# Dummy products on TensorE during the routing of a mixture-of-experts layer

## Chip, cores and metric

The kernel runs on one core of a Trainium2 chip. The metric is the device time of one execution in microseconds (us), median of several runs. All tensors are f32.

## What is computed

One decoder layer for 512 tokens of width 1024: a mixing stage (block-sparse attention and an RWKV-7 recurrence), a cross-attention into 256 memory tokens, and a mixture of 32 experts, each followed by a residual and a layer norm. The change lies at the passage from the second norm to the experts:

```python
x = layer_norm(DEEPNORM_ALPHA * x + memory_cross_attention(x, mem, w_mem_q[l], w_mem_kv[l], w_mem_o[l]),
               ln_g[l, 1], ln_b[l, 1])
xf = x.reshape(B * S, D)
e_idx, gate = route(xf, w_router, b_router)     # sigmoid scores; best group of 4; top 2 in it
y = moe_ffn(xf, e_idx, gate.astype(x.dtype), w_exp_gate[l], w_exp_up[l], w_exp_down[l])
x = layer_norm(DEEPNORM_ALPHA * x + y.reshape(B, S, D), ln_g[l, 2], ln_b[l, 2])

def expert_block(args):
    xb, e = args
    h = jax.nn.silu(xb @ w_gate[e]) * (xb @ w_up[e])
    return h @ w_down[e]
```

Each expert's three matrices are 2 MB each, 6 MB in all, so 192 MB of weights pass through the core.

## The kernel before

**The routing block** (L1638 to L1843). TensorE multiplies the output projection of the cross-attention (L1709, 64 products of 128x128 weights with 512 columns), turns the normed tokens (L1692, `tokens`), multiplies them with the router (L1699, `logits`) and turns the 32 x 512 logits (L1726). VectorE then picks the group and the two experts of each token (L1780 to L1811; its result is `oh`, signalled by `oh_done`). TensorE counts with two products how many tokens stand before each one in its expert's list (L1731, L1732, `rk_full`). VectorE makes the weights of the two experts (L1814 to L1821), the place of each token in its expert's list (L1828 to L1834) and the 0/1 matrix `hit` (L1384, `hits_done`). TensorE multiplies that in eight products of 96 columns, the table product (L1390), and VectorE copies the result to `tabs` (L1397 to L1399): for each expert, up to 64 token numbers, row numbers and weights. This ends the block for TensorE and VectorE. SyncE has issued expert loads meanwhile: experts 0, 1 and 2 have a buffer each, filled by then.

**The expert block** (L1920 on). SyncE loads the norm's parameters (L175, two loads), then the weights from expert 3 on, in halves of 1 MB (`load_half`, L1419). A load may be issued when TensorE has read the same part of the expert three before (`w_read`, L1931) and when the fourth load before it has landed (L1933). The first half of expert 3's gate and up weights thus waits for the first half of expert 0's gate and up products. GpSimd clears a buffer (L1983), gathers the 64 rows of an expert (L1969) and later scatters its results (L1974). TensorE, for each expert e: 32 instructions of gate and up products (L2042, in two halves of 16), transposes of the next expert's tokens (L2026, L2027), transposes of the hidden values (the same lines), and 16 instructions of the down projection (L2051). The last expert's result is not scattered but added by products (L2125).

The names used below: `bank[7]` is an accumulation bank that is free between the copy of L1772 and the transposes of L2086; `x1` holds the normed tokens, `ident` a unit matrix.

Of the kernel before, what the change touches and what calls it, by code (L numbers as in the profile page):

```python
# [54 lines left out]
def hybrid_decoder_trunk(nc, x, x_t, mem_t, params, w_in, w_decay_up, w_iclr_up, w_gate_up, w_out, w_mem_q, w_mem_kv, w_mem_o, w_router,  # L55
                         b_router, w_exp_gate, w_exp_up, w_exp_down, ln_g, ln_b, out):
    ctx = ExitStack()
    with ctx:
        def sb(name, shape, dt=F32):
            return ctx.enter_context(nc.sbuf_tensor(name, shape, dt))  # L60
# [14 lines left out]
        def link(eng, ins):  # L75
# [9 lines left out]
        bank = ([tpair[:, i, :] for i in range(2)] + [cpair[:, i, :] for i in range(2)]  # L85
                + [ctx.enter_context(nc.psum_tensor(f"bank{i}", [P, 512], F32)) for i in range(4, 8)])

        ident = sb("ident", [P, P])
# [31 lines left out]
        x1 = keys[:, :, :, :].rearrange("p a j s -> p (a j s)").rearrange("p (t d) -> p t d", t=NT)  # L121
# [7 lines left out]
        def slot(g, width):  # L129
            s = slot_of(g)  # L130
            buf = avq[:, :] if s == 2 else ring[:, s * SLOT:(s + 1) * SLOT]
            return buf[:, 0:KT * width].rearrange("p (k n) -> p k n", k=KT)
# [26 lines left out]
        def group_here(eng, g):  # L159
            eng.wait_ge(w_here[slot_of(g)], 16 * uses_of_slot(g))  # L160
# [48 lines left out]
        with A:  # L209
# [15 lines left out]
            with A1:  # L225
# [55 lines left out]
                with nc.Block() as block:  # L281
                    @block.sync
                    def _(sp):
                        gl = slot(GL, 2 * P)
                        for h, (here, done) in enumerate(((x_here[0], gl_half), (x_here[1], w_here[slot_of(GL)]))):
                            ks = slice(4 * h, 4 * h + 4)
                            sp.dma_start(gl[:, ks, :], groups[GL][:, ks, :]).then_inc(done, 16)
                            sp.dma_start(xT[:, ks, :], x_t[:, ks, :]).then_inc(here, 16)
                        load_group(sp, GK)
                        sp.dma_start(wup[0:64, :], w_decay_up[0]).then_inc(up_here, 16)  # L290
                        sp.dma_start(wup[64:128, :], w_iclr_up[0]).then_inc(up_here, 16)
                        sp.dma_start(wg[:, :], w_gate_up[0]).then_inc(up_here, 16)
                        for g, last in ((GR, ("L", 1)), (GV, ("K", 3)), (GAV, ("R", 3)), (GAQ, ("V", 3))):
                            load_group(sp, g, (job_full, jobs.index(last) + 1))
# [194 lines left out]
            with A2:  # L489
                def s2(name, shape, dt=F32):  # L490
# [52 lines left out]
                         + [("K", i) for i in range(KT // 2)]  # L543
                         + [("V", i) for i in range(2 * MT)])
                fill_units = [(f, part) for f, (kind, _) in enumerate(fills)
                              for part in range(1 if kind in ("bon", "gate") else 8)]
                early_units = sum(fills[f][0] not in ("K", "V") for f, _ in fill_units)
# [43 lines left out]
                for r in range(ROUNDS):  # L591
                    n, k = divmod(r, RPI)
# [795 lines left out]
        def table_product(pe):  # L1388
            for kt in range(TOP_K * NT):
                last = nc.tensor.matmul(bank[6][:, 0:3 * NE], hit[:, kt, :],  # L1390
                                        sel_rows[:, kt // NT, kt % NT, :, :].rearrange("p f e -> p (f e)"),
                                        start=(kt == 0), stop=(kt == TOP_K * NT - 1))
            last.then_inc(tab_full, 1)
# [35 lines left out]
        with B:  # L1429
# [208 lines left out]
            with nc.Block() as block:  # L1638
# [45 lines left out]
                @block.tensor  # L1684
                def _(pe):
                    def tokens(t):

                        pe.wait_ge(n2.shifted, t + 1)
                        for hf in range(2):
                            for k in range(4):  # L1690
                                c = 4 * hf + k
                                last = nc.tensor.transpose(bank[2 * t + hf][:, k * P:(k + 1) * P],  # L1692
                                                           x1[:, t, c:D:KT], ident[:, :])
                            last.then_inc(t2_full, 1)

                    def logits(t):

                        for k in range(KT):
                            last = nc.tensor.matmul(bank[0][0:NE, t * P:(t + 1) * P], wr[:, k, :],  # L1699
                                                    x2T[:, k, t * P:(t + 1) * P], start=(k == 0), stop=(k == KT - 1))  # L1700
                        return last

                    group_here(pe, GMO)
                    group_here(pe, GMO + 1)
                    for t in range(NT):
                        for hf in range(2):
                            w = slot(GMO + hf, 512)
                            for k in range(KT):
                                last = nc.tensor.matmul(bank[2 * t + hf][:, :], omT[:, k, t * P:(t + 1) * P],  # L1709
                                                        w[:, k, :], start=(k == 0), stop=(k == KT - 1))  # L1710
                            last.then_inc(mo2_full, 1)
                        if t >= 2:
                            tokens(t - 2)
                    tokens(NT - 2)
                    pe.wait_ge(router_here, 32)
                    for t in range(NT - 1):
                        pe.wait_ge(t2_act, 2 * t + 2)
                        logits(t)
                    tokens(NT - 1)
                    pe.wait_ge(t2_act, 2 * NT - 1)  # L1720
                    pe.wait_ge(t2_dve, 1)
                    last = logits(NT - 1)
                    last.then_inc(lg_full, 1)
                    pe.wait_ge(lg_read, 1)
                    for t in range(NT):
                        last = nc.tensor.transpose(bank[1][:, t * NE:(t + 1) * NE], lg[:, t * P:(t + 1) * P],  # L1726
                                                   ident[0:NE, 0:NE])
                    last.then_inc(lt_full, 1)

                    pe.wait_ge(oh_done, 1)  # L1730
                    nc.tensor.matmul(bank[2][:, 0:P], before[:, :], oh[:, 2, :, :], start=True, stop=True)  # L1731
                    nc.tensor.matmul(bank[2][:, P:2 * P], ones[:, :], oh[:, 2, :, :], start=True, stop=True)\  # L1732
                        .then_inc(rk_full, 1)
                    pe.wait_ge(hits_done, 1)
                    pe.wait_ge(ids_done, 2)
                    table_product(pe)

                @block.scalar
                def _(act):
# [572 lines left out]
```

## Time and profile before

| what | value |
|---|---|
| median of 3 runs | 1179.37 us (1179.17 to 1180.02) |
| profiled execution | 1179.95 us, its span 1178.1 us |
| TensorE busy (matmul) | 1049.1 us, 89% |
| VectorE, ScalarE, GpSimd busy | 329.5, 244.7, 85.1 us |
| mean granted clock of TensorE | 0.97 |
| DMA moved | 262.83 MB, mean 223 GB/s |
| the chain that ended last | DMA 28%, PE 14%, DVE 2% of the span |

Times in the trace count from the span's start. The routing lies between 629 and 650 us, the expert block behind it.
### The profile page before, as it was taken

What the parts mean: (1) busy time and instruction counts of PE and PEld (TensorE: products, weight loads), DVE (VectorE), ACT (ScalarE), POOL (GpSimd) and SP (SyncE); (2) the same over time, 40 slices, a digit from 0 to 9 for tenths busy, and PEclk for the clock granted to TensorE, in tenths of its full rate; (3) what the DMA queues carried; (4) which work ended last, traced back from release to release, by engine and by line L of the source; (5) the groups of instructions that cost most, each with busy time, mean ns of one, the idle gap of its engine ahead of it and who ended that gap; (6) DMA issues with size and microseconds to landing.
All of it is one profiled execution on the core that took longest, in us unless ns stands there. A gap on an engine that the chain in (4) does not pass through costs nothing. (4 is left out here: it accounts for less than half of the span.)

```text
span 1178.1 us, 15678 instructions
## 1 busy us (share of the span) xinstructions
PE 1049.1 (89%) x6604; PEld 525.7 (45%) x6604; DVE 329.5 (28%) x705; ACT 244.7 (21%) x494; POOL 85.1 (7%) x130
## 2 busy tenths in 40 slices
PE   7999899999899999998995799999987778898876
PEld 3444445567655544565444344434333333333332
DVE  0179522234665453004236100100000000000007
ACT  2431122234445401024001111111110111011112
POOL 2000100000000000000000311111111101111000
PEclk9999899999999999999997799999999999989997
DMA  7112120222104402720309599999999999999994
GB/s 252 47 51 100 70 73 2 73 73 74 42 33 144 179 1 70 286 105 40 112 1 352 221 406 408 401 406 398 400 393 390 397 384 395 389 405 401 400 371 179
DMA packets 55382, 262.83 MB, mean 223 GB/s; under 512 B 7170, under 2 KB 8322, under 8 KB 30352
## 3 DMA queue, kind: packets, MB, share of 16 engines
q1 hardware_dynamic: 50048, 253.39, 55.6%
q0 software_dynamic: 5120, 8.40, 2.2%
q8 instruction: 53, 0.87, 0.3%
q14 instruction: 17, 0.14, 0.0%
q10 hardware_dynamic: 144, 0.02, 0.0%
HBM read 257.60 MB, written 12.58 MB: 229 GB/s over the span
## 5 line engine op out<-in xcount | busy, mean ns | idle before, releaser
L2042 PE MATMUL tpair<-ring,xgT 128*64 128x512 f32 x352 | 82.9, 619 | 13.1 <-DMA ring<-in_w_exp_up 12.4
L2206 DVE TENSOR_TENSOR hb<-cpair,sil 64x512 f32<-64x512 f32 x21 | 14.6, 693 | 276.6 <-ACT sil L2146 276.6
L2042 PE MATMUL cpair<-ring,xgT 128*64 128x512 f32 x352 | 78.9, 595 | 13.7 <-DMA ring<-in_w_exp_up 13.1
L2042 PE MATMUL cpair<-xT,xgT 128*64 128x512 f32 x160 | 71.5, 594 | 15.1 <-DMA ar<-in_w_exp_up 15.1
L2042 PE MATMUL cpair<-ar,xgT 128*64 128x512 f32 x160 | 71.8, 596 | 0.0
L1974 POOL DMA_INDIRECT y_rows<-ye,tabs x32 | 32.5, 1015 | 410.8 <-ACT ye L2154 410.0
L900 PE MATMUL bank<-xT,ring 128*128 128x512 f32 x128 | 60.3, 605 | 0.0
L2042 PEld LDWEIGHTS tpair<-ring,xgT 128*64 128x64 f32 x352 | 27.5, 142 | 67.0 <-issue 66.1
L2042 PEld LDWEIGHTS cpair<-ring,xgT 128*64 128x64 f32 x352 | 26.4, 137 | 64.1 <-issue 63.3
L2154 ACT ACTIVATE ye<-bank,tabs 128x512 f32<-128x512 f32 x31 | 21.3, 687 | 155.2 <-PE bank L2051 155.2
L2051 PE MATMUL bank<-avq,hT 128*64 128x512 f32 x176 | 46.3, 674 | 5.7 <-DVE hT L2210 5.7
L2206 DVE TENSOR_TENSOR hb<-tpair,sil 64x512 f32<-64x512 f32 x11 | 7.6, 693 | 147.1 <-ACT sil L2146 147.1
L2042 PEld LDWEIGHTS cpair<-xT,xgT 128*64 128x64 f32 x160 | 21.0, 137 | 62.0 <-issue 62.0
L345 PE MATMUL bank<-xT,ring 128*128 128x512 f32 x112 | 48.5, 593 | 0.0
L2051 PE MATMUL bank<-ring,hT 128*64 128x512 f32 x176 | 41.8, 618 | 5.7 <-DVE hT L2210 5.7
L2146 ACT ACTIVATE sil<-cpair 64x512 f32<-64x512 f32 x21 | 12.4, 591 | 162.6 <-PE cpair L2042 162.6
L2051 PE MATMUL bank<-mixT,hT 128*64 128x512 f32 x160 | 39.7, 643 | 5.2 <-DVE hT L2210 5.2
L919 PE MATMUL tpair<-ring,mixT 128*128 128x512 f32 x96 | 42.0, 593 | 0.0
L345 PE MATMUL tpair<-xT,ring 128*128 128x512 f32 x64 | 29.5, 621 | 7.8 <-DMA xT<-in_x_t 7.8
L991 ACT ACTIVATE pcb<-tpair 128x512 f32<-128x512 f32 (+1 forms) x32 | 17.4, 544 | 90.0 <-DVE pcb L1159 89.9
L345 PEld LDWEIGHTS bank<-xT,ring 128*128 128x128 f32 x112 | 21.2, 190 | 27.1 <-issue 26.3
L2027 PEld LDWEIGHTS tpair<-ident,xg 64*128 64x128 f32 x224 | 32.5, 225 | 0.0
(389 smaller groups left out, 1619.9 us busy)
## 6 DMA issues: line engine op xcount, KB each, us to landing
ring<-in_w_exp_gate SPq DMA_DIRECT2D x44, 1024.0 KB, 10.1
ring<-in_w_exp_up SPq DMA_DIRECT2D x44, 1024.0 KB, 10.3
ring<-in_w_exp_down SPq DMA_DIRECT2D x22, 1024.0 KB, 11.1
avq<-in_w_exp_down SPq DMA_DIRECT2D x22, 1024.0 KB, 11.2
xT<-in_w_exp_gate SPq DMA_DIRECT2D x20, 1024.0 KB, 11.6
ar<-in_w_exp_up SPq DMA_DIRECT2D x20, 1024.0 KB, 11.2
mixT<-in_w_exp_down SPq DMA_DIRECT2D x20, 1024.0 KB, 11.6
ring<-in_w_in SPq DMA_DIRECT2D x6, 2048.0 KB, 8.2
```

Source lines behind the costliest of these rows:

```text
L345: last = nc.tensor.matmul(dst[:, :], w[:, k, j * P:(j + 1) * P], xT[:, k, :], start=(k == 0), stop=(k == KT - 1))
L900: last = nc.tensor.matmul(dst[:, :], lhs, rhs, start=(k == 0), stop=(k == KT - 1))
L919: last = nc.tensor.matmul(wo_bank[i % 3][:, :], mixT[:, k, t * P:(t + 1) * P], slot(GO + hf, 512)[:, k, :], start=(k == 0), stop=(k == 2 * ...
L991: return nc.scalar.activation(dst, src, ACT.Copy, **kw)
L1974: return pool.indirect_dma_start(y_rows[:, :], bass.IndirectOffsetOnAxis(idx.bitcast(U32), 0), src, None, bounds_check=below(TOP_K * S * 2 ...
L2027: return nc.tensor.transpose(dst, src, ident[0:CAP, 0:CAP])
L2042: last = nc.tensor.matmul(bank[1 + s][m * CAP:(m + 1) * CAP, :], xgT[:, k, :], expert_slot(s, m)[:, k * DE:(k + 1) * DE], start=(k == 0), ...
L2051: last = nc.tensor.matmul(bank[5][m * CAP:(m + 1) * CAP, :], hT[:, k, :], expert_slot(s, 2)[:, o:o + 512], start=(k == 0), stop=(k == FT - 1))
L2146: nc.scalar.activation(sil[:, :], bank[1 + e % 3][0:CAP, :], ACT.Silu).then_inc(sil_done, 1)
L2154: nc.scalar.activation(ye[:, e % 3, :], bank[5][:, :], ACT.Copy, scale=tabs[:, e, 2:3].bitcast(F32)).then_inc(y_scaled, 1)
L2206: V.tensor_tensor(hb[:, :], bank[1 + e % 3][CAP:P, :], sil[:, :], ALU.mult).then_inc(h_done, 1)
```

## The change

TensorE gets three groups of products in the routing block: eight after the transposes of the logits, ahead of its wait for `oh_done`; four after the two counting products, ahead of its waits for `hit` and `sel_rows`; six after the table product, as its last instructions of the block. They multiply `ident` with 512 columns of `x1` into bank 7; nothing reads the result, and the bank is overwritten in the next block.

```diff
                     last.then_inc(lt_full, 1)
 
+                    def kept_busy(n):
+
+                        for _ in range(n):
+                            nc.tensor.matmul(bank[7][:, :], ident[:, :], x1[:, 0, 0:512], start=True, stop=True)
+
+                    kept_busy(8)
                     pe.wait_ge(oh_done, 1)
                     nc.tensor.matmul(bank[2][:, 0:P], before[:, :], oh[:, 2, :, :], start=True, stop=True)
                     nc.tensor.matmul(bank[2][:, P:2 * P], ones[:, :], oh[:, 2, :, :], start=True, stop=True)\
                         .then_inc(rk_full, 1)
+                    kept_busy(4)
                     pe.wait_ge(hits_done, 1)
                     pe.wait_ge(ids_done, 2)
                     table_product(pe)
+                    kept_busy(6)
```

## Rows read from the trace of the kernel before

**Rows 1.** The page, the span in 40 slices: granted clock and DMA share, in tenths.

```profile
PEclk9999899999999999999997799999999999989997
DMA  7112120222104402720309599999999999999994
```

**Rows 2.** Busy time by stretch: length, PE, PEld, DVE, ACT, POOL, clock, DMA share, GB/s.

```profile
633.00:635.00 2.00, 0.00 (x0) 0.00 (x0) 1.79 (x9) 0.00 (x0) 0.00 (x0) 1.00 1.01 414
635.00:636.00 1.00, 0.00 (x0) 0.00 (x0) 0.87 (x4) 0.00 (x0) 0.00 (x0) 0.84 1.04 426
...
645.00:650.00 5.00, 3.73 (x16) 3.49 (x16) 1.62 (x10) 0.00 (x0) 0.00 (x0) 0.50 0.62 259
...
663.00:665.00 2.00, 2.00 (x12) 0.67 (x10) 0.00 (x0) 0.00 (x0) 0.00 (x0) 1.00 0.14 45
```

**Rows 3.** Timeline, routing and expert 0: start, length, engine, line, tiles, idle before.

```profile
631.86 0.43 PE L1726 MATMUL tpair<-ident,lg 32*128 32x32 f32 x4 [0.77 <-DVE lg L1776]
639.85 0.79 PE L1731 MATMUL cpair<-oh,before 128*128 128x128 f32 x2 [7.56 <-DVE oh L1811]
...
645.37 3.73 PE L1390 MATMUL bank<-sel_rows,hit 128*128 128x96 f32 x16 [4.30 <-DVE hit L1384]
...
656.41 0.74 PE L2026 MATMUL tpair<-ident,xg 64*128 64x64 f32 x2 [7.32 <-DMA xg<-xs_rows,tabs]
...
658.59 5.82 PE L2042 MATMUL tpair<-ring,xgT 128*64 128x512 f32 x16 [0.69 <-ACT xgT L2141]
```

**Rows 4.** The SP queue's waits (total us, times, longest), and its timeline.

```profile
SPq L1419 <- PE tpair L2042: 15.8, 2, 13.6
...
664.46 0.33 SPq L1419 DMA_DIRECT2D ring<-in_w_exp_gate  x1
```

**Rows 5.** The chain that ended last, in order of time: start, length, what.

```profile
784.42 6.76 PE tpair L2042 x31
791.18 11.17 DMA ar<-in_w_exp_up
...
1126.17 3.67 PE tpair L2042 x16
```

**Rows 6.** TensorE's timeline: rows at full clock in the shapes of the new products.

```profile
513.56 3.73 PE L1466 MATMUL tpair<-ar,avq 128*128 128x128 f32 x32
...
570.96 7.03 PE L1709 MATMUL tpair<-avq,ar 128*128 128x512 f32 x16
577.83 7.03 PE L1709 MATMUL cpair<-ring,ar 128*128 128x512 f32 x16
```

**Rows 7.** VectorE's timeline in the routing.

```profile
639.50 0.29 DVE L1811 TENSOR_TENSOR oh<-oh 128x128 f32<-128x128 f32 x1
...
642.05 0.09 DVE L1828 MEMSET sc<- 128x32 f32 x1
...
644.09 1.23 DVE L1384 TENSOR_TENSOR hit<-caps,place 128x1024 f32<-128x1024 f32 x1
```

**Rows 8.** The end of the routing block: timeline, and the SP queue's wait.

```profile
649.47 0.20 DVE L1399 COPY tabs<-bank 128x32 f32<-128x32 f32 x1
649.94 0.33 SPq L175 DMA_DIRECT2D kT<-in_ln_g  x1
...
SPq L1638 <- PEq L1638: 10.6, 1, 10.6
```

**Rows 9.** Down projections of experts 26, 30 and 31 (timeline), and the clock there.

```profile
1068.17 5.35 PE L2051 MATMUL bank<-mixT,hT 128*64 128x512 f32 x16 [0.52 <-DVE hT L2210]
...
1132.76 3.65 PE L2051 MATMUL bank<-ring,hT 128*64 128x512 f32 x16 [0.52 <-DVE hT L2210]
...
1146.98 0.68 PE L2026 MATMUL bank<-ident,hb 64*128 64x64 f32 x2 [1.42 <-DVE hb L2206]
...
1148.56 6.59 PE L2051 MATMUL bank<-avq,hT 128*64 128x512 f32 x16 [0.52 <-DVE hT L2210]
...
1148.00:1154.00 6.00, 5.48 (x15) 1.72 (x16) 4.78 (x5) 0.00 (x0) 0.00 (x0) 0.50 1.02 414
```

## Prediction, made before the changed kernel was run

> **What bounds the kernel now.** I read the views in this order. First the page's slices: the granted clock dips in two neighbouring slices just before the long stretch in which the DMA share is nine tenths or more [rows 1]. Then the busy time in short stretches [rows 2]: the clock is 1.00 up to 635, falls between 635 and 636 (the mean there is 0.84, which puts the fall at 635.7) and stands at 0.50, that is 1.2 GHz, through the routing; from 663 it is 1.00, 2.4 GHz, again. Then TensorE's timeline of the same time [rows 3]: it has been idle since 632.3, waits 7.56 us for `oh`, 4.30 us for `hit` and 7.32 us for the first gather.
>
> Whether the end depends on this stretch is read from the SP queue and from the chain that ended last. The six loads for expert 3 can start only when TensorE has read the first half of expert 0's gate and up weights: the queue waited 13.6 us for the tpair product and issued at 664.46 [rows 4]. The chain runs through TensorE's products up to 791, and from there to 1126 it is one load after another, after which it passes to TensorE's last two experts [rows 5]. In its first part TensorE and the loads are both full (the DMA share is nine tenths or more in all those slices too), so from 664 to 1126 the stream of loads has one length, and the end moves by what **the issue at 664.46** moves. Ahead of that issue stands one path: the routing on VectorE, the table product, the end of the block, the first gather, expert 0. Behind 1126 stands TensorE's own tail.
>
> **The change, part by part.** Three groups of dummy products are added, eight, four and six. Each product has the shape of one of L1709: 128x128 weights, 512 columns, f32. Sixteen instructions, which are eight products, start 6.87 us after the sixteen before them and last 7.03 us [rows 6]: 0.86 us each at full clock, with 0.16 us of tail behind the last. Nothing is removed. The dummies read `ident` and `x1` and write bank 7, whose last reader (the copy of L1772) has been waited for already, so no wait is added and only TensorE has anything queued behind them. No DMA and no POOL instruction is added or moved.
>
> *Eight before the wait for `oh`.* They start where the transposes of `lg` end, at 632.3, and take 7.03 us: 639.3. The wait ends at 639.8 [rows 3, 7], so there are 0.5 us of cover. Should they overrun, VectorE reads the rank products only behind its memset at 642.05 [rows 7], and they ended at 641.06: 1.0 us more. Price: nothing. What they bring is that the clock should not fall at 635.7.
>
> *Four after the rank products.* At full clock those end at about 640.5; 4 x 0.86 = 3.4 us take us to 644.0, and `hit` is there at 645.3 [rows 7]. Price: nothing, with 1.3 us of cover.
>
> *The table product.* Its sixteen instructions took 3.73 us at half clock [rows 3]. The nearest row at full clock has 32 instructions with 128x128 weights and 128 columns in 3.73 us, tail included [rows 6]: (3.73 - 0.16) / 2 = 1.79 us for sixteen (here only 96 columns, but as many weights to load). The product then ends at 647.2 instead of 649.1, **1.9 us earlier**; this is what the full clock can give the routing.
>
> *Six after the table product.* They stand between it and the end of the block. Before, the last work ahead of that end was VectorE's copy of the tables, done at 649.67, and SP's first instruction of the next block came at 649.94, 0.27 us later; its wait of 10.6 us at the line of the block is put down to TensorE's queue [rows 8]. I take it that the end of a block waits until every engine has finished all it was given. The six then end at 647.16 + 6 x 0.86 + 0.16 = 652.47, and the release comes at 652.74 against 649.94: **2.8 us later**. The 1.9 us are already in this: the product is done earlier, but 5.3 us that nobody reads stand behind it, on the path. Everything of the next block shifts along: the memset of `xg`, the gather, which goes on sharing the rings with the two `ln` loads (they shift too), the transposes at 656.41, expert 0 at 658.59.
>
> *Expert 0.* Its first sixteen instructions took 5.82 us [rows 3], against 3.65 us for sixteen at full clock [rows 9]. Bounds: 2.2 us gained if the clock is up throughout, 2 x 3.65 = 7.3 us, 1.5 us lost, if it is down throughout. TensorE will be idle from 652.5 to 659.2, 6.7 us: nearly the 7.32 us of before, and more than the 3.5 us of idling after which the clock fell at 635.7 [rows 2, 3]. So the clock should fall before the token transposes and return some microseconds into expert 0, as before. I take **0**, the row as it is.
>
> *The tail.* The last down projection took 6.59 us, nearly all of it at clock 0.50; the same sixteen instructions one expert earlier took 3.65 us, and expert 26's 5.35 us [rows 9]. The work before them is alike, so where such a fall lands is a matter of timing, and a shift of some microseconds may move it. Bounds: 2.9 us gained, nothing lost (it is the longest row of this line). I take the middle kind, 5.2 us: **1.4 us gained**.
>
> **The sum:** 2.8 + 0 - 1.4 = +1.4 us. The profiled execution took 1179.95 us (a span of 1178.1 and 1.85 us around it), so it would take 1181.4; it stands 0.6 us above the median of the runs, 1179.37, and against that the forecast is **1180.8**.
>
> **A page against the trace.** The trace shows the clock at 1.00 until 3.5 us after TensorE's last work and then at 0.50 [rows 2, 3]. The Trainium skill, "TensorE: Matmul & The Clock Gate", section "Why this matters for your kernels", advises against long pauses between bursts of products, since throughput drops after them; the trace agrees. It is the case for this change, and is silent on what filling costs ahead of a block's end. The same page, section "Step-by-step: what each phase is for", says that the sequencer does not wait for a product to drain but takes the next instruction. By that rule TensorE's queue could reach the end of the block while the dummies still run, which is rival 2; no row shows it, because before each block's end here the last product has a reader that ends later.
>
> **The rivals.**
>
> 1. *The clock falls inside the filled stretch (slower).* Between the four dummies (644.0) and the table product (645.4) 1.4 us stay open, and ahead of the last down projection the clock fell around a gap of 1.42 us with small products behind it [rows 9], not after a long pause. If it falls at 645 or 646, the table product and the dummies are charged at half clock. The 5.35 us row lost 1.7 us, the 6.59 us row 2.9 us against 3.65 us; here all of it would lie ahead of the block's end: +2.8 + 1.7 - 1.4 = +3.1, 1182.5, up to 1183.7 with the longer fall. It decides from the moment at which the clock is below 1.00 anywhere between 645 and 652. For it: falls beside short gaps do occur. Against it: dense products up to 644. Chance 0.22; 0.03 of it is that the filling doesn't hold the clock in the first wait either, which would be the change not doing what it says (but the clock was still 1.00 where the first dummy starts).
>
> 2. *The block's end does not wait for the dummies (faster).* Then it waits for VectorE: 647.3, plus 0.57 us for the tables (649.10 to 649.67), plus 0.27, gives 648.1, 1.8 us earlier than before. The gather then lands at 654.6, TensorE has idled 2.1 us only, and expert 0's first half takes 3.65 us, 2.2 us less. With the tail: -1.8 - 2.2 - 1.4 = -5.4, 1174.0; 1175.4 with the tail as it was. For it: the dummies have no reader. Against it: the blocks' ends seen so far followed the last work of every engine. Chance 0.13.
>
> 3. *The end waits, yet expert 0 has the full clock, or has it back sooner.* Up to 2.2 us come back: 2.8 - 2.2 - 1.4 = -0.8, 1178.6. For it: the token transposes may bring the clock up earlier than they did. Against it: 6.7 us of idling. Chance 0.15.
>
> The forecast itself keeps 0.5; its own range is 1179.3 (last down projection at 3.65 us) to 1182.2 (as before).
>
> **How the numbers follow.** A measurement of this kernel can tell about 0.2% from no change, 2.4 us: below 1177.0 is faster, above 1181.7 slower. Faster is rival 2 and a small part of rival 3 (with the shortest tail): 0.17. Slower is rival 1 and the part of the forecast in which the tail stays as long as it was, 0.12: 0.34. The rest, 0.49, lies within. The range leaves out rival 2 and little at the upper end: 1176.4 to 1184.0.
>
> **What would show each step.** In the new profile: the clock at 1.00 from 629 to beyond 652 (below it near 645: rival 1); the table product at 1.8 to 2 us; twelve instructions of dummies right behind it, and SP's first instruction of the next block 0.3 us after the last of them, at 652.7 (rival 2: at 648.1, with dummies still running); the first load of expert 3 issued at 667.3; the clock below 1.00 between 656 and 666; the chain made of loads until about 1129; the length of the last down projection. The forecast is wrong if that first load is not 2.8 us later, or if the stream behind it takes another time than 1126.2 - 664.5 = 461.7 us.

## The result, and the profile after

The changed kernel took 1184.49 us (median of 8 runs, 1181.22 to 1186.75), the kernel before beside it on the same chip 1179.2 us (1177.6 to 1182.69). The ratio is 1.0036, with a 95% interval of 1.002 to 1.0053: **slower by 4.2 us**, between 2.4 and 6.2. (Ratios and intervals, here and below, are the recorded ones; the quotient of two medians differs from them by up to 0.0014, here it is 1.0045.) Times 1179.37 us, the ratio gives 1183.6; forecast were 1180.8, in a range from 1176.4 to 1184.0, and "slower" had 0.34 against 0.49 for "within 0.2%". The profiled execution took 1184.29 us, its span 1182.4 us.

The page's slices of the changed kernel, granted clock and DMA share, answer to [rows 1]:

```profile
PEclk9999899999999999999999789999999999999998
DMA  7112120222113402630309599999999999999984
```

There is still a dip in the clock, but it now stands one slice later. Busy time by stretch in the changed kernel (columns as in [rows 2]):

```profile
629.00:647.00 18.00, 15.25 (x63) 8.53 (x64) 12.95 (x47) 1.01 (x2) 1.23 (x2) 1.00 1.01 387
647.00:652.50 5.50, 5.50 (x15) 2.28 (x14) 0.47 (x3) 0.00 (x0) 0.00 (x0) 1.00 0.19 80
652.50:656.00 3.50, 0.00 (x1) 0.00 (x0) 3.09 (x7) 0.00 (x0) 2.25 (x3) 1.00 0.63 227
656.00:657.00 1.00, 0.00 (x0) 0.00 (x0) 0.96 (x2) 0.00 (x0) 0.83 (x1) 0.72 0.89 295
657.00:666.00 9.00, 6.40 (x21) 2.78 (x23) 0.29 (x1) 1.88 (x2) 5.58 (x9) 0.50 0.18 54
```

The clock is held through the whole routing, as the change wants. Then it falls all the same, at 656.4, 3.9 us after the last dummy, and is at half rate through the token transposes and the first products of expert 0. The timeline shows why TensorE had nothing to do then (line numbers of the new file: L1733 are the dummies, L2050 is the old L2042, L2059 the old L2051, L1977 the old L1969; it answers to [rows 3] and [rows 8]):

```profile
631.79 0.43 PE L1726 MATMUL tpair<-ident,lg 32*128 32x32 f32 x4 [0.77 <-DVE lg L1784]
632.15 7.13 PE L1733 MATMUL bank<-keys,ident 128*128 128x512 f32 x16
...
640.34 3.60 PE L1733 MATMUL bank<-keys,ident 128*128 128x512 f32 x8
...
645.30 2.02 PE L1390 MATMUL bank<-sel_rows,hit 128*128 128x96 f32 x16 [1.36 <-DVE hit L1384]
...
647.16 5.34 PE L1733 MATMUL bank<-keys,ident 128*128 128x512 f32 x12
...
647.70 0.20 DVE L1399 COPY tabs<-bank 128x32 f32<-128x32 f32 x1
652.75 0.33 SPq L175 DMA_DIRECT2D kT<-in_ln_g  x1
...
658.91 0.73 PE L2034 MATMUL tpair<-ident,xg 64*128 64x64 f32 x2 [6.41 <-DMA xg<-xs_rows,tabs]
...
667.55 0.33 SPq L1419 DMA_DIRECT2D ring<-in_w_exp_gate  x1
```

VectorE has the tables ready at 647.90, 1.8 us earlier than before. Nobody can use them: the next block begins at 652.75, 0.25 us after the last dummy. The SP queue's waits (total, times, longest) put that down to TensorE, 13.3 us against the 10.6 us of [rows 8]:

```profile
SPq L1638 <- PEq L1638: 13.3, 1, 13.3
```

The instructions of the block's end (L1638) show the wait itself. This is TensorE's drain instruction in the changed kernel and in the kernel before, with its length in ns and its start:

```profile
L1638 PEldq DRAIN  x1: 6013/6013/6013, 646.5 to 646.5; - x1
...
L1638 PEldq DRAIN  x1: 3702/3702/3702, 645.4 to 645.4; - x1
```

TensorE's queue was at the drain at 646.5, before the first of the six started (647.16), and the drain stood until 652.5, when the last one ended. In the kernel before it stood until 649.1, the end of the table product.

The chain that ended last, at its end, answers to [rows 5] and [rows 9]:

```profile
1120.09 9.88 DMA ring<-in_w_exp_up
...
1130.10 3.67 PE tpair L2050 x16
...
1136.70 5.35 PE bank L2059 x16
...
1154.15 5.38 PE bank L2059 x16
```

The 4.3 us between the two spans can be laid out on these marks. The routing began 0.07 us earlier. From L1726 to the next block: 20.96 us against 18.08, +2.88. From there to the first transposes: 6.16 against 6.47, -0.31 (why is not shown: in neither kernel was an expert load still running, the DMA moved nothing in the last microsecond before the block; the four kernels with six or twelve dummies ahead of the block's end have 6.11 to 6.16 here, and the six others whose transposes wait for the gather 6.47 to 7.14). From the transposes to the first load of expert 3: 8.64 against 8.05, +0.59, all of it in expert 0's first half, 6.5 us instead of 5.9 from its start to the load. **Together +3.09 at that load**, 667.55 against 664.46. The stream from it to the last product that waits for a load: 462.55 us against 461.71, +0.84. The down projection of expert 30: 5.35 us against 3.65, +1.7. The last one: 5.38 against 6.62, -1.24. These make +4.39; the rest of the tail gives 0.1 back.

### The profile page after: what moved, and what is told of

Its sections match the earlier page's. It is cut to its first block and busy times, and to the rows that moved or that the text cites. A ratio compares the mean times of both kernels' runs of the same rounds, so it can differ in the third digit from the quotient of the medians.

```text
span 1182.4 us, 15750 instructions
## 1 busy us (share of the span) xinstructions
PE 1063.1 (90%) x6640; PEld 530.3 (45%) x6640; DVE 330.1 (28%) x705; ACT 244.7 (21%) x494; POOL 84.8 (7%) x130
## 5 line engine op out<-in xcount | busy, mean ns | idle before, releaser
L2050 PE MATMUL tpair<-ring,xgT 128*64 128x512 f32 x352 | 81.8, 612 | 16.5 <-DMA ring<-in_w_exp_up 15.8
L2050 PE MATMUL cpair<-ring,xgT 128*64 128x512 f32 x352 | 78.9, 595 | 14.6 <-DMA ring<-in_w_exp_up 13.9
L2050 PE MATMUL cpair<-xT,xgT 128*64 128x512 f32 x160 | 71.5, 593 | 12.4 <-DMA ar<-in_w_exp_up 12.4
L2050 PE MATMUL cpair<-ar,xgT 128*64 128x512 f32 x160 | 71.8, 595 | 0.0
L2050 PEld LDWEIGHTS tpair<-ring,xgT 128*64 128x64 f32 x352 | 27.0, 141 | 69.7 <-issue 68.8
L2050 PEld LDWEIGHTS cpair<-ring,xgT 128*64 128x64 f32 x352 | 26.2, 137 | 65.0 <-issue 64.2
L2059 PE MATMUL bank<-avq,hT 128*64 128x512 f32 x176 | 46.5, 677 | 5.7 <-DVE hT L2218 5.7
L2059 PE MATMUL bank<-ring,hT 128*64 128x512 f32 x176 | 43.4, 638 | 5.7 <-DVE hT L2218 5.7
L2050 PEld LDWEIGHTS cpair<-xT,xgT 128*64 128x64 f32 x160 | 21.1, 137 | 59.2 <-issue 59.2
L2059 PE MATMUL bank<-mixT,hT 128*64 128x512 f32 x160 | 39.6, 641 | 5.2 <-DVE hT L2218 5.2
## 6 DMA issues: line engine op xcount, KB each, us to landing
ring<-in_w_exp_gate SPq DMA_DIRECT2D x44, 1024.0 KB, 10.7
ring<-in_w_exp_up SPq DMA_DIRECT2D x44, 1024.0 KB, 10.2
xT<-in_w_exp_gate SPq DMA_DIRECT2D x20, 1024.0 KB, 10.6
```

The lines of the kernel that those rows point to most:

```text
L2050: last = nc.tensor.matmul(bank[1 + s][m * CAP:(m + 1) * CAP, :], xgT[:, k, :], expert_slot(s, m)[:, k * DE:(k + 1) * DE], start=(k == 0), ...
L2059: last = nc.tensor.matmul(bank[5][m * CAP:(m + 1) * CAP, :], hT[:, k, :], expert_slot(s, 2)[:, o:o + 512], start=(k == 0), stop=(k == FT - 1))
```

## The experiments

Each kernel was profiled once and timed against the kernel before, which ran 23 to 35 times in each series. One thing has to be known for reading them: identical code ahead of the routing took between 631.6 and 635.7 us in the twelve profiles up to L1726 (more on that in the last section). So marks are counted from L1726, and those of the profiles are sharper than the medians, whose intervals are 1.5 to 2.5 us to either side. The marks of all kernels:

| kernel | next block, from L1726 | first transposes, from L1726 | first load of expert 3, from L1726 | stream | last two down projections | ratio (95%) |
|---|---|---|---|---|---|---|
| before | 18.08 | 24.55 | 32.60 | 461.7 | 3.65, 6.59 | 1 |
| changed | 20.96 | 27.12 | 35.76 | 462.6 | 5.35, 5.35 | 1.0036 (1.002 to 1.0053) |
| changed again | 20.96 | 27.12 | 35.82 | 463.5 | 5.35, 5.22 | 1.0029 (1.0015 to 1.0043) |
| without six | 16.37 | 22.99 | 31.73 | 462.9 | 5.35, 5.35 | 0.9974 (0.9956 to 0.9992) |
| six in next block | 16.37 | 23.02 | 30.54 | no wait there | 3.65, 5.35 | 0.9967 (0.9947 to 0.9988) |
| twelve | 26.11 | 32.22 | 40.08 | 459.6 | 5.23, 5.10 | 1.0054 (1.0035 to 1.0074) |
| only next block | 18.07 | 26.49 | 32.32 | 459.9 | 5.30, 5.14 | 0.9995 (0.9981 to 1.001) |
| gaps filled | 16.36 | 22.59 | 28.42 | 463.2 | 5.35, 5.35 | 0.9982 (0.9965 to 0.9999) |
| gaps and tail | 16.37 | 23.35 | 29.17 | 462.6 | 3.65, 3.65 | 0.996 (0.9947 to 0.9973) |
| tail only | 18.07 | 25.21 | 32.94 | no wait there | 3.65, 3.65 | 0.9997 (0.9982 to 1.0013) |
| early experts | 16.39 | 23.08 | 28.91 | 459.4 | 3.65, 3.65 | 0.9965 (0.9949 to 0.9981) |
| changed, early | 20.96 | 27.11 | 35.55 | 460.4 | 5.13, 5.05 | 1.0029 (1.0012 to 1.0046) |

("Stream" is the time from the first load of expert 3 to the second half of expert 30's gate and up products, where these wait for a load. All times in us.)

**The changed kernel again.**

> The changed kernel itself, beside its variants on one chip. Theory (the six products after the table product hold the end of the block, since every engine must have finished): the next block's first SP instruction at 652.7, 2.8 us later than before, the first load of expert 3 issued about 3 us later than 664.5, the time 3 to 4.5 us above before. Rival (the loss in the first profile comes from where the clock fell in the two last experts, and is not the same from run to run): the block's end as before the change plus 2.8 us all the same, but a time anywhere from 0 to 5 us above before.

1183.75 us. The marks up to the next block are the same to 0.01 us, and both down projections again ran partly at half clock. What the changed kernel loses is not a matter of one execution.

**Without the six.**

```diff
                     table_product(pe)
-                    kept_busy(6)
```

> The eight and the four stay, the six after the table product are left out. Theory: the block ends 0.27 us after VectorE's copy of the tables, next block from 648.1, 4.6 us earlier than in the changed kernel and 1.8 us earlier than before; TensorE then idles 7 us, so expert 0 starts at half clock and its first half takes 5 to 7 us; time 1177 to 1178, 1 to 2.5 us below before. Rival (it is the eight or the four that cost, through the clock or VectorE's reads): the time stays above before.

1177.95 us, against 1183.75 us for the changed kernel in the same series. The next block begins 16.37 us behind L1726: 1.71 us earlier than before, 4.59 us earlier than in the changed kernel. The eight and the four cost nothing and bring the 1.7 us of the table product; the six cost 4.6. The slowness of the changed kernel is in the six, the rival is out. Expert 0 then started at half clock, as expected, and took 6.56 us for its first half: 0.7 us of the gain went there. The first load of expert 3 was 0.9 us ahead of before, and the stream and the two last down projections took 1.2 and 0.5 us more, so in the profiles nothing is left of the gain: from L1726 to the end 547.0 us against 546.2. The ratio of the times, 0.9974, lies below 1 by little more than its interval.

**Twelve instead of six.**

```diff
-                    kept_busy(6)
+                    kept_busy(12)
```

> Twelve products after the table product instead of six. Theory: each costs 0.86 us on the path, so the next block begins 5.15 us later than in the changed kernel, at 657.9, and the time is 5 us above the changed kernel, 8 to 9.5 above before. Rival (the end of the block waits only until the products have been handed to TensorE, and the six happened to end at that moment): the next block begins less than 5.15 us later.

```profile
647.32 10.49 PE L1733 MATMUL bank<-keys,ident 128*128 128x512 f32 x24
...
658.05 0.33 SPq L175 DMA_DIRECT2D kT<-in_ln_g  x1
```

The timeline of that kernel: the next block begins 26.11 us behind L1726, exactly 5.15 us later than with six, and 0.24 us after the last product. The end of this block waits for products without a reader, to the last one. The time was 1185.99 us, only 2.2 us above the changed kernel where 5 were expected. The profile says where the rest is: expert 0's first half was 0.8 us faster (5.68 against 6.46 to 6.53) and the stream 459.6 us instead of 462.6 to 463.5. Why the stream was shorter is taken up below.

**The six in the next block.**

```diff
-                    kept_busy(6)
...
+                for _ in range(6):
+                    nc.tensor.matmul(bank[7][:, :], ident[:, :], x1[:, 0, 0:512], start=True, stop=True)
                 tokens(0)
                 for e in range(LAST):
```

> The eight and the four stay; the six are moved behind the end of the block, ahead of TensorE's wait for the first gather. Theory: next block from 648.1; the six run from 648.2 to 653.4 beside POOL and the gather, which lands near 654.6; the clock is 1.00 at expert 0, whose first sixteen instructions take 3.65 us; first load of expert 3 issued at 660.5, 4.0 us earlier than before; time 1175 to 1175.5, that is 4 us below before and 8 below the changed kernel. Rival (the clock in expert 0 is not worth anything because the stream of loads is bound elsewhere): issue at 660.5 but the time only 1.8 us below before.

The same six products, placed behind the end of the block instead of ahead of it: 1176.54 us, 7.2 us below the changed kernel in the same series. Against the kernel without them it is 1.4 us less, with intervals that overlap (0.9947 to 0.9988, 0.9956 to 0.9992): that the six are worth anything here is not shown by the times. The profiles have the first load 1.2 us earlier than without them. They run beside the gather:

```profile
652.07 0.33 SPq L175 DMA_DIRECT2D kT<-in_ln_g  x1
...
652.12 5.39 PE L2085 MATMUL bank<-keys,ident 128*128 128x512 f32 x12 [0.90 <-PEq L1638]
658.72 0.69 PE L2033 MATMUL tpair<-ident,xg 64*128 64x64 f32 x2 [1.21 <-DMA xg<-xs_rows,tabs]
...
660.85 8.78 PE L2049 MATMUL tpair<-ring,xgT 128*64 128x512 f32 x32 [0.69 <-ACT xgT L2150]
```

But expert 0's first half took 5.39 us, not 3.65: the clock was 1.00 until 661 and fell then, behind the two gaps of 1.21 and 0.69 us. The load was issued at 30.54, not 28.6. Half of the theory held (the block's end), half failed (the clock in expert 0).

**The gaps filled.** As the kernel with the six moved, but with seven products ahead of the token transposes and one of 256 columns behind them (`idle_fill` issues such products, one for each number of columns that it is given):

```diff
+                idle_fill(*[512] * 7)
                 tokens(0)
+                idle_fill(256)
                 for e in range(LAST):
```

> As the run with the six moved, but seven products ahead of the wait for the gather and a half product (256 columns) between the token transposes and expert 0, so that the gaps of 1.21 and 0.69 us that were left there are filled. Theory (the fall at 661.3 us in that run came from those gaps): the clock stays at 1.00 through expert 0, its first half takes 3.65 us instead of 5.4, the first load of expert 3 is issued 28.8 to 29.3 us behind L1726 instead of 30.5, and the time is 1 to 2 us below that run. Rival (the gaps are too short to matter, the fall has another origin): the clock falls there all the same.

```profile
648.83 6.25 PE L2086 MATMUL bank<-keys,ident 128*128 128x512 f32 x14 [0.90 <-PEq L1638]
655.00 0.69 PE L2033 MATMUL tpair<-ident,xg 64*128 64x64 f32 x2
...
657.13 7.09 PE L2049 MATMUL tpair<-ring,xgT 128*64 128x512 f32 x32
```

With the gaps closed all 32 instructions ran at full clock, the first half in 3.70 us, and the first load of expert 3 was issued 28.42 us behind L1726: 4.2 us earlier than before, 7.3 earlier than in the changed kernel. The mechanism is as the theory had it. The time was not: 1178.05 us, no better than with the gaps open, against the 1 to 2 us expected. In its profile the clock fell ten microseconds later, in expert 0's down projection, and the stream took 463.2 us.

**Only the six in the next block.** The kernel before, with this alone:

```diff
+                for _ in range(6):
+                    nc.tensor.matmul(bank[7][:, :], ident[:, :], x1[:, 0, 0:512], start=True, stop=True)
                 tokens(0)
                 for e in range(LAST):
```

> The kernel before, with only the six products in the expert block, ahead of the wait for the first gather (no eight, no four, none after the table product). Counted from the transposes of the logits (L1726). Theory: the routing is as before, next block 18.1 us behind L1726 and not 16.4; the six start at half clock, take 7 to 10 us and end beyond the landing of the first gather (6.5 us behind the block's start), so that expert 0 starts up to 3 us later but at full clock; time within 2 us of before. Rival (the eight and the four do nothing, the gain of the run without six and of the run with the six moved is chance): the same times as the run with the six moved, 2.8 us below before.

The table product was at half clock again (3.73 us), and the six took 8.43 us instead of 5.39, since the clock was at 0.50 for the first six microseconds of them; the transposes waited for them, to 26.49 us. Expert 0 then ran at full clock, and the first load stood at 32.32, 0.3 us ahead of before. 1178.59 us, a ratio of 0.9995: as the theory had it, nothing won (the interval reaches down to 0.9981, so the times alone do not part this kernel from the one with all three groups; the marks do). The eight and the four carry 1.7 us in the routing, and more behind it, since the clock is then up when the six begin.

**The tail.** The waits of the last two experts (behind gate and up, behind the hidden transposes, behind the last token transposes) filled with products of 512 and 256 columns; together with the filled gaps, and alone. A part of the edit:

```diff
+                idle_fill(256, src=combT)
                 gate_up(LAST)
+                idle_fill(512, 256, src=combT)
                 down(LAST)
```

> As the run with the gaps filled, and products of 512 and 256 columns in the waits of the last two experts (behind gate and up, behind the hidden transposes, behind the last token transposes). Theory (the falls at the tail follow from those waits of 1.4, 0.5 and 0.7 us): no down projection of the last two experts above 3.7 us, time 2 to 4 us below the run with the gaps filled. Rival (the filling itself delays the products behind it as much as the clock gives back): the down projections at 3.65 us, the time unchanged.

> The kernel before with only the filling of the last two experts' waits. Theory: everything up to the last two experts as before, both last down projections at 3.65 us, time 1.5 to 3.5 us below before. Rival: as for the run with gaps and tail, no gain.

Both profiles show each of the last two down projections at 3.65 us. In the first kernel the tail runs thus (timeline):

```profile
1131.21 3.65 PE L2058 MATMUL bank<-ring,hT 128*64 128x512 f32 x16
...
1147.00 3.65 PE L2058 MATMUL bank<-avq,hT 128*64 128x512 f32 x16
```

Its time was 1174.67 us, ratio 0.996: 3.4 us below the kernel with the gaps alone, 4.0 below before, **the lowest median here, and faster than both kernels** (with the six moved, 0.9967, and with the early experts, 0.9965, its interval overlaps). But the tail alone gave 1178.48 us, ratio 0.9997, where 1.5 to 3.5 us were expected; its interval reaches down to 0.9982, 2.1 us. That filling keeps the clock up in the tail is shown; that it is worth 2 to 3 us by itself is not. In the profile of the tail alone the adding of the last expert's result (L2257, here L2269) begins 28.3 us behind the second half of expert 30's gate and up products, against 31.1 us before; so the gain stands in that profile and not in the median. Little more is to be had from TensorE there: in both kernels the chain that ended last now leaves it behind expert 30 for the scatter of its result and the loads that read it back, in the first kernel thus:

```profile
1136.43 6.34 DMA y_rows<-ye,tabs
...
1143.31 7.26 DMA xT<-y_rows
```

**The early experts.** In five profiles the clock fell within 10 us behind the first load of expert 3, and there the stream lasted 462.6 to 463.5 us; in the three others in which it can be read it lasted 459.6 to 461.7 (with the six moved no product waited there, which puts it at 460.8 at most). Two kernels, the one with gaps and tail filled and the changed one, test whether one makes the other, with a product of 256 columns added in the wait of 0.52 us ahead of the down projections of experts 0 to 3:

```diff
                     turned_hidden().then_inc(ht_full, 1)
+                    if e < 4:
+                        nc.tensor.matmul(bank[6][:, 0:256], ident[:, :], x1[:, 0, 0:256], start=True, stop=True)
```

> As the run with gaps and tail filled, and a product of 256 columns in the wait of 0.52 us ahead of the down projection of experts 0 to 3. In five profiles (the changed kernel twice, without six, gaps filled, gaps and tail) the clock fell within 10 us behind the first load of expert 3, and the stream from that load to the last wait for a load lasted 462.5 to 463.5 us; in the four others without such a fall 459.6 to 461.7. Theory (the fall delays TensorE's reads and starves the stream): no fall between 660 and 700 us, stream 459.6 to 461.7, time 1 to 2 us below the run with gaps and tail. Rival (the stream's length varies by itself): the fall is gone and the stream still takes 462.5 or more, the time unchanged.

> The changed kernel with that same product in experts 0 to 3. Theory: the first load of expert 3 at 35.8 us behind L1726 as in the changed kernel, stream 459.6 to 461.7 instead of 462.5 to 463.5, time 1 to 2 us below the changed kernel and still 2 to 3 us above before, what the end of the block costs. Rival: the time is the changed kernel's.

Behind the first load of expert 3 the clock stayed up in both (in the second it was down from 659.5 to 669.4, ahead of that load at 670.32). From the first kernel's stretch table (columns as in [rows 2]):

```profile
629.00:660.00 31.00, 26.12 (x106) 14.44 (x105) 18.48 (x59) 3.26 (x5) 7.70 (x9) 1.00 0.83 316
660.00:700.00 40.00, 39.87 (x192) 17.41 (x190) 3.35 (x6) 6.20 (x10) 6.13 (x9) 1.00 0.93 367
```

and the streams were 459.4 and 460.4 us, where the theory wanted them. That makes ten profiles in which the two go together. The rows also show the way from one to the other. The next loads into expert 0's buffer, those of the down weights, wait for its down projection. The SP queue's waits for the down projections, in the changed kernel and in the kernel before:

```profile
SPq L1419 <- PE bank L2059: 13.0, 8, 4.7
...
SPq L1419 <- PE bank L2051: 6.8, 7, 3.3
```

The longest of these waits is 4.2 to 4.7 us in the five profiles with the fall and 2.9 to 3.3 us in the seven others; the down weights are issued 9.8 to 9.9 us behind the first load instead of 8.3 to 8.4. In the first 25 us behind that load the DMA moved 8.8 to 9.1 MB with the fall and 9.5 to 9.8 MB without, and half a megabyte is an estimated 1.2 us at the 418 GB/s of these stretches. The medians did not follow: 1175.03 us (ratio 0.9965) against 1174.67 (0.996) without the product, and 1183.61 us against 1183.75 (1.0029 both). So the link between the fall and the stream is shown in the profiles, about 1 us of it with its cause; what it is worth in time is below what these runs can show, or absent. This stays open.

## Why the prediction was right, and where not

**The path.** Right for the changed kernel: 3.1 of its 4.3 us stand at the first load of expert 3 and came through the stations named. That the end moves by what this load moves does not hold in general. With the gaps filled the load came 4.2 us earlier than before and the end, counted from L1726, 2.3 us; the stream and the tail took the rest.

**Eight, four, and the table product.** Right to a tenth. The eight ended at 639.3, the wait for `oh` at 639.8; the table product's sixteen instructions took 1.86 us start to start against 1.79. Without the six the routing was 1.71 us shorter.

**Six ahead of the block's end: +2.8.** Right. The release was forecast at 652.74 and came at 652.75; twelve products moved it by another 5.15 us. Rival 2 is dead: no engine passed the end of this block before TensorE's last product. The rule of the Trainium skill ("TensorE: Matmul & The Clock Gate", "Step-by-step: what each phase is for") that the sequencer goes on without waiting for a product agrees with the trace up to the drain, which the queue reached at 646.5, and the drain then stood for 6.0 us until the products were done. The prediction says that no row of before could show this; its drain at 645.4, held for 3.70 us to the end of the table product, was such a row. Rival 1 did not come: the clock was 1.00 through the gap at 645.

**Expert 0: 0.** Right in kind: the clock fell in the 6.4 us of idling and came back in expert 0. The size was +0.6 us in the first profile (0.7 in the repeat), within the bound of 1.5. The first transposes, taken to follow the block's start by the same time, came 0.3 us sooner behind it.

**The tail: -1.4.** This is the step that failed, and with it the size of the sum. I compared the last down projection's 6.59 us with a middle row, and left the one before it, 3.65 us, as it was. They belong together: both stand behind the same waits and both lie on the chain. Before: 3.65 + 6.59 = 10.2 us. Changed: 5.35 + 5.35 = 10.7. Unfilled, in nine profiles: 9.0 once, and 10.2 to 10.7 eight times. So a stretch at half clock in the tail is the rule, the kernel before was no bad case, and the term should have been 0 to +0.5. With it the sum would have been +2.8 to +3.3, 1182.2 to 1182.7, and "slower" the likeliest case. Of the 3.0 us between the forecast +1.4 and the profile's +4.4, this term is 1.9.

**The stream.** Taken as a constant 461.7 us, and another length was named as a sign of a wrong forecast; it was 462.6 in the first profile, and 459.4 to 463.5 in all. Its spread is as large as most effects studied here, and was missing from the range.

**The range.** That it held the result was luck. The forecast's own path was given up to 1182.2, and the measured 1183.6 lies above that. The upper end of 1184.0 was there for rival 1, which did not come; the room left for it was filled by the tail and the stream.

## What to carry to other kernels

Products that nobody reads are free only while somebody else is late: count them against the wait that they stand in, and never put them ahead of a point at which all engines meet, since that point waits for them as for any other work. The same six products cost 4.6 us ahead of the block's end and nothing behind it, where the gather is waited for. The kernels that keep the eight and the four and have their other fillings in waits behind the block's end were 0.2 to 0.4% faster than before, and the eight and the four alone gave 0.26%; whether the further fillings add to that lies within the intervals. And before judging a saving in the middle, lay out the marks behind it (here the first load, the stream, the last two experts), because the stream and the last two experts vary by as much as the saving.

## What the runs showed of the hardware that I had not expected

*The clock can fall beside short waits too.* In the kernel with the six moved it fell at 661.5 after gaps of only 1.21 and 0.69 us with small transposes between them; with 0.43 and 0.86 us products in those gaps it did not. In the last two experts, with waits of 1.4 and 0.5 us around small transposes, it fell at least once in each of nine profiles, and with the waits filled in none of three. The short waits are not enough by themselves: the same wait of 0.52 us stands ahead of expert 0's down projection in the kernel before, which took 3.65 us. What decides is not shown.

*Where it falls differs between executions of the same instructions, and the time goes with it.* Up to L1726 all kernels have the same instructions. The kernel before was at half clock at 130 to 137 and 465 to 468 us and came to L1726 at 631.86. The kernel with the six moved, in its profiled execution, had a third such stretch at 313 to 316 and a longer one at 466 to 473, and came there at 635.70. Its stretches:

```profile
460.00:466.00 6.00, 4.21 (x18) 2.38 (x17) 0.89 (x2) 1.09 (x2) 0.00 (x0) 1.00 0.00 0
466.00:474.00 8.00, 7.27 (x19) 4.22 (x19) 4.00 (x7) 1.24 (x3) 0.00 (x0) 0.57 0.85 273
```

Up to L1726 that is 17 us at half clock against 10.2 us, and 3.8 us between the two executions, nearly the whole effect of the change, from code that the change does not touch. The twelve profiles follow this: 631.6 to 632.8 us in the eight with 10.2 us at half clock, 634.3 to 634.9 in the three with 13.6, 635.7 in this one.
